# Expert layers of an encoder kernel: splitting the activations before the transposes instead of after them

## The reference, cut to what matters

```python
def swiglu(x, w1, w3, w2):
    return (jax.nn.silu(x @ w1) * (x @ w3)) @ w2

for e in range(N_EXPERTS):          # 8 experts, EXPERT_DIM = 3584
    out = out + combine[..., e:e + 1] * swiglu(x, w1[e], w3[e], w2[e])
```

## Time and profile before

| | |
|---|---|
| median of three runs | 2157.66 us |
| profiled execution, its own time | 2154.84 us |
| its span | 2152.8 us |
| PE busy | 2107.4 us (98%) |
| DVE busy | 1684.3 us (78%) |
| ACT busy | 1323.0 us (61%) |
| granted TensorE clock, mean | 0.988 of full speed |
| experts, from the first to the last transpose | 1083.7 to 2093.2 us |
| one pass of an expert | 127.2 us |

### The profile page before, as it was taken

The page is one execution under the profiler, slowest core; times in us unless marked ns, Lnnn a source line. Parts: engine busy times, 40 slices in busy tenths (PEclk is TensorE's granted clock), DMA queues, the critical chain, the costliest instruction groups (busy, mean ns, idle before and its releaser), DMA issues.

```text
span 2152.8 us, 37035 instructions
## 1 busy us (share of the span) xinstructions
PE 2107.4 (98%) x13496; PEld 1888.2 (88%) x13496; DVE 1684.3 (78%) x2376; ACT 1323.0 (61%) x1864; POOL 24.2 (1%) x45
## 2 busy tenths in 40 slices
PE   8999999899999999999899999999999999999997
PEld 7999999899999999999888888888888888888886
DVE  4998766655457998766588888998888898888885
ACT  5546654444445456545377777777777777777773
POOL 0000100000000000100000000000000000000000
PEclk9999999999999999999899999999999999999999
DMA  7535435355355434453489898998989889898971
GB/s 253 192 116 170 147 135 218 139 214 191 121 197 165 173 118 152 147 196 118 155 320 365 333 350 333 350 365 334 354 341 347 342 341 371 325 356 335 347 305 77
DMA packets 74964, 533.17 MB, mean 248 GB/s; under 512 B 8655, under 2 KB 8655, under 8 KB 11000
## 3 DMA queue, kind: packets, MB, share of 16 engines
q1 hardware_dynamic: 72620, 525.04, 64.2%
q0 software_dynamic: 2048, 6.29, 1.6%
q10 hardware_dynamic: 204, 0.54, 0.1%
HBM read 530.74 MB, written 1.10 MB: 247 GB/s over the span
## 4 chain that ended last, share of the span: by engine, by line
PE 95%; DVE 3%; ACT 1%; DMA 1%; issue 0%; SPq 0%; DVEq 0%; ACTq 0%
PE ps L887 28%; PE ps L889 28%; PE ps L888 28%; PE ps L557 4%; PE ps L1069 1%; PE ps L1098 1%; PE ps L841 1%; PE ps L869 1%; PE ps L753 1%; PE ps L856 1%; DVE xn L1719 0%; DMA constants_sb<-constants 0%; DVE rstd L1713 0%; DVE wlo L2105 0%; PE ps L563 0%; DMA ring<-w_ple 0%
## 5 line engine op out<-in xcount | busy, mean ns | idle before, releaser
L2105 DVE TENSOR_TENSOR wlo<-ring,whi 128x1024 fp32r<-128x1024 f32 x746 | 872.6, 1219 | 144.1 <-ACT whi L1540 143.6
L1540 ACT ACTIVATE whi<-ring 128x1024 fp32r<-128x1024 f32 x746 | 749.3, 1055 | 141.4 <-PE ps L889 130.6
L887 PE MATMUL ps<-whi,xhi 128*128 128x512 f32 (+1 forms) x1160 | 439.4, 379 | 1.0 <-DVE xlo L2227 1.0
L889 PE MATMUL ps<-whi,xlo 128*128 128x512 f32 (+1 forms) x1160 | 430.0, 371 | 0.0
L888 PE MATMUL ps<-wlo,xhi 128*128 128x512 f32 x904 | 356.8, 395 | 0.0
L887 PE MATMUL ps<-xhi,whi 128*128 128x256 f32 x960 | 272.3, 284 | 2.2 <-DVE gt L2127 1.4
L888 PE MATMUL ps<-xlo,whi 128*128 128x256 f32 x960 | 268.0, 279 | 0.0
L889 PEld LDWEIGHTS ps<-whi,xlo 128*128 128x128 f32 x1160 | 219.0, 189 | 40.5
L889 PE MATMUL ps<-xhi,ring_lo 128*128 128x256 f32 x896 | 251.5, 281 | 0.0
L887 PEld LDWEIGHTS ps<-whi,xhi 128*128 128x128 f32 x1160 | 219.4, 189 | 35.6 <-DVE xlo L2227 1.4
L888 PEld LDWEIGHTS ps<-wlo,xhi 128*128 128x128 f32 x904 | 170.3, 188 | 35.9
(11 more groups left out here) (298 smaller groups left out, 3801.3 us busy)
## 6 DMA issues: line engine op xcount, KB each, us to landing
ring<-w_experts SPq DMA_DIRECT2D x340, 1024.0 KB, 4.9
ring<-w_mixers SPq DMA_DIRECT2D x114, 1024.0 KB, 4.9
ring<-w_dense SPq DMA_DIRECT2D x33, 1024.0 KB, 4.8
ring<-w_ple SPq DMA_DIRECT2D x10, 1024.0 KB, 4.9
bias<-bias_rows POOLq DMA_DIRECT2D x8, 256.0 KB, 7.0
cvfa<-bias_rows POOLq DMA_DIRECT2D x8, 256.0 KB, 5.4
constants_sb<-constants SPq DMA_DIRECT2D x1, 1048.0 KB, 9.0
h<-x_in SPq DMA_DIRECT2D x1, 1024.0 KB, 4.9
```

The lines of the kernel that those rows point to most:

```text
L887: pe.matmul(dst, lhs[0], rhs[0], start=first, stop=False, skip_group_check=True)
L889: return pe.matmul(dst, lhs[1], rhs[0], start=False, stop=last, skip_group_check=True)
L1540: act.activation(whi[:, slot, :], ring[:, j % RING, lo:lo + UNIT], ACT.Copy).then_inc(s_wh, 1)
L2105: dve.tensor_tensor(wlo[:, slot, :], ring[:, j % RING, lo:lo + UNIT], whi[:, slot, :], ALU.subtract).then_inc(s_wl, 1)
```

## The change

The hidden values are split before the transposes, by slot: ACT copies `hid` to `hid_high` in fp32r, DVE subtracts to get `hid_low`. PE then turns both by ordinary fp32r products with a unit matrix (`ident_r`), four of 128 moving columns, instead of the two fp32 transposes. One ACT copy of 128 x 512 takes both parts out of PSUM; the subtraction `hlo` from PSUM is gone. The PE waits on `s_hm` and `s_hl` become waits on `s_sl` and `s_hb`. ACT now waits for `s_hm` between units 0 and 1, and DVE for `s_sh` before unit 0.

```diff
-        hhi = sb("hhi", [P, 2, 2, SEQ], F32R)
-        hlo = sb("hlo", [P, 2, 2, SEQ], F32R)
+        hhl = sb("hidden_high_low", [P, 2, 2, 2, SEQ], F32R)
+        hhi, hlo = hhl[:, 0, :, :, :], hhl[:, 1, :, :, :]
+        hid_high = sb("hidden_high_by_slot", [P, SEQ], F32R)
+        hid_low = sb("hidden_low_by_slot", [P, SEQ], F32R)
+        ident_r = sb("ident_r", [P, P], F32R)
...
@@ PE, step
                             if u == 1:
-                                pe.wait_ge(s_hm, c0 + k + 1)
-                                for half in range(2):
-                                    m = pe.transpose(bank(2 + cc % 2, half * P, P), gt[:, 0, half * P:half * P + P],
-                                                     con("ident"))
+                                pe.wait_ge(s_sl, c0 + k + (1 - DENSE_CHUNKS))
+                                for part in range(2):
+                                    for half in range(2):
+                                        m = pe.matmul(bank(2 + cc % 2, part * SEQ + half * P, P),
+                                                      (hid_high, hid_low)[part][:, half * P:half * P + P],
+                                                      ident_r[:, :], start=True, stop=True)
                                 m.then_inc(s_ht, 1)
...
-                        pe.wait_ge(s_hl, c0 + k + 1)
+                        pe.wait_ge(s_hb, c0 + k + (1 - DENSE_CHUNKS))
@@ ACT, route
+                act.activation(ident_r[:, :], con("ident"), ACT.Copy).then_inc(s_id, 1)
@@ ACT, chunk
-                        highs(u0 + (k * 6 + 4), 2, 2, rr, j)
+                        high(u0 + (k * 6 + 4), 2, 0, rr, j)
+                        act.wait_ge(s_hm, c0 + k + 1)
+                        act.activation(hid_high[:, :], hid[:, 0, :], ACT.Copy).then_inc(s_sh, 1)
+                        high(u0 + (k * 6 + 4), 2, 1, rr, j)
...
-                        act.activation(hhi[:, cc % 2, :, 0:P], bank(2 + cc % 2, 0, SEQ).rearrange(
-                            "p (h t) -> p h t", h=2), ACT.Copy).then_inc(s_hh, 1)
+                        act.activation(hhl[:, :, cc % 2, :, 0:P], bank(2 + cc % 2).rearrange(
+                            "p (a h t) -> p a h t", a=2, h=2), ACT.Copy).then_inc(s_hb, 1)
@@ DVE, chunk
                         dve.tensor_tensor(hid[:, 0, :], hs[:, 0, :], bank(cc % 2, SEQ, SEQ), ALU.mult).then_inc(s_hm, 1)
+                        dve.wait_ge(s_sh, c0 + k + (1 - DENSE_CHUNKS))
+                        dve.tensor_tensor(hid_low[:, :], hid[:, 0, :], hid_high[:, :], ALU.subtract).then_inc(s_sl, 1)
                         lows(u0 + (k * 6 + 4), 2, 2, j)
-                        dve.wait_ge(s_hh, c0 + k + 1)
-                        dve.tensor_tensor(hlo[:, cc % 2, :, 0:P], bank(2 + cc % 2, 0, SEQ).rearrange(
-                            "p (h t) -> p h t", h=2), hhi[:, cc % 2, :, 0:P], ALU.subtract).then_inc(s_hl, 1)
```

More of the change, by code:

```diff
@@ L381, in trunk_program @@
         s_ht = sem("hidden_transposed")
+        s_sh = sem("slot_hidden_high")
+        s_sl = sem("slot_hidden_low")
+        s_id = sem("ident_rounded")
+        s_hb = sem("hidden_parts_by_feature")
         s_hh = sem("hidden_hi")
@@ L1082, in experts @@
                     up_unit(0, u, 0, DENSE_UNITS)
+                pe.wait_ge(s_id, 1)
                 with pe.Fori(0, n_p) as q:
```

## The result

The changed kernel takes 2192.62 us (four runs, 2192.03 to 2194.36), the kernel before 2156.05 us (four runs): 1.0174 times as long, 95% interval 1.0162 to 1.0186. The forecast was 2193 us. The profiled execution took 2192.73 us, 37.9 more than the one before (2154.84).

What follows compares the result with a forecast made beforehand. PE's stream was taken to bound the expert stretch. Products 25.2, waits 9.2 and 2.4, and tail 0.2 sum to 37.0 us on 2154.84; with half of 2.8 added, 2193 us, range 2178 to 2245 (90%).

Steps and rivals of the forecast that it cites:

- What bounds the kernel: Expert stretch of 1010 us: each microsecond of PE's stream counts, ACT and DVE savings nothing; 2.5 us lost to PE's sequencer.
- The pair of transposes: The two fp32 transposes removed from each of 112 chunks: 0.227 us per pair, 0.113 for one.
- The price of a short product: Four new fp32r products per chunk at p = 0.113 us each, set by the weight load; 25.2 us more in all.
- The lower bound (columns): Short product priced by moving columns only: 0.059 us each, 1.0 us more over 112 chunks.
- the upper one (full format): Short product as dear as a full-format one: p = 0.226 us, 75.8 us more; as a rival 2244 us, 16%.
- The factor of four for transpose mode: Skill's claim for FP32, by which a plain fp32 product would cost 0.45 us; the prediction read 0.226 from the trace.
- The hand-over: ACT copy and DVE subtraction before PE's turn: operand 0.96 us later after `gt`; chunk 0 waits 1.15 us, 9.2 us in all.
- Chunk 1: Second chunk of each pass: operand ready 0.3 us late, eight times, 2.4 us; known only within 0 to 0.7.
- The ring in the middle chunks: Closed ring of waits from PE's products through ACT and DVE back to PE: 8.36 us against PE's 8.77, nothing charged.
- The rival C: The ring closes in every chunk, 0.1 to 0.3 us open in 96 further chunks: 2203 to 2222 us, 9%.
- The tail: End of the last pass, through `whi`, `wlo` and a transfer: the longer copy adds 0.2 us.
- The sum: 25.2 + 9.2 + 2.4 + 0.2 = 37.0 us on the profiled 2154.84, with half of 2.8 added: 2193 us.

Runs made afterwards that it cites:

- the run with plain products: Kernel before with a plain fp32 product with the unit matrix in place of each transpose, two per chunk; 2179.44 us, 1.0115 times the kernel before.
- the two halvings: Changed kernel with 64 instead of 128 moving columns in the four products, 2192.31 us; with 64 instead of 128 stationary columns, 2171.03 us.
- the products alone: Changed kernel without the hand-over: DVE writes the fp32r tile directly, all four products turn it, low part left out; 2182.78 us, 1.0122 times the kernel before.
- when it was opened: Changed kernel with two more same-size subtractions into spare tiles ahead of the one PE waits for; 2207.78 us, 1.0244 times the kernel before.
- the hand-over run: Changed kernel with the two old fp32 transposes of `gt` in place of the four products, all waits kept; 2164.08 us, 1.0043 times the kernel before.

## Why the prediction was right

**What bounds the kernel.** Right: all that was lost is PE's stream or PE's waits. ACT's busy time grew by 60 us, and of that only the copy ahead of a waiting PE counts. One reading was wrong: the 2.5 us that the prediction gives to PE's sequencer are waits for `hlo` in chunk 0, as shown above. The change takes them away, a gain of some 1.4 us that no term of the sum has.

**The pair of transposes.** Its 0.227 us fits the run with plain products, which cost twice as much, as worked out.

**The price of a short product.** The step that carried the forecast: p = 0.113 from rows of fp32 products with 16, 64 and 128 moving columns, on the ground that their common part is the load. Measured 0.117, and by the two halvings the load is the ground. 112 x 0.24 is 26.9 us for 25.2 forecast; 1.4 of it returned, since the gap in chunk 0 closed, and 25.5 is what the products alone cost. The lower bound (columns) and the upper one (full format) were both far off, so what chose between them mattered more than either. The section LDWEIGHTS of TensorE: Matmul & The Clock Gate in the Trainium skill gives columns / 1.2 ns for a load, an estimate of 107 and 53 ns for 128 and 64 columns. The runs agree nearly by the distances between loads, 0.108 to 0.112 and 0.057 to 0.062 us, and roughly by the price of a product as taken above, 0.117 and 0.069. The factor of four for transpose mode with FP32 in the section Terms of the same page of the Trainium skill, weighed in the prediction, is refuted here: the runs show 0.227 for the pair and 0.45 for the plain products, a factor of two.

**The hand-over.** Chunk 0 of the second pass, to be set beside the earlier trace rows:

```profile
1216.47 0.42 DVE L2261 TENSOR_TENSOR gt<-gs,ps 128x256 f32<-128x256 f32 x1 [1.16 <-ACT gs L1624]
...
1217.29 0.41 ACT L1627 ACTIVATE hidden_high_by_slot<-gt 128x256 fp32r<-128x256 f32 x1
...
1217.72 0.42 DVE L2263 TENSOR_TENSOR hidden_low_by_slot<-gt,hidden_high_by_slot 128x256 fp32r<-128x256 f32 x1 [0.83 <-ACT hidden_high_by_slot L1627]
...
1218.20 0.30 PEld L1107 LDWEIGHTS ps<-ident_r,hidden_high_by_slot 128*128 128x128 f32 x2 [1.18 <-DVE hidden_low_by_slot L2263]
```

From the start of `gt` to PE's load it is 1.73 us; the prediction had 1.74 (1210.31 to 1212.05), with the copy behind unit 0 as it said. The load waits 1.18 us for 1.15 forecast. Chunk 1 waits 0.5 by its load for 0.3, in the stated 0 to 0.7. But the two waits do not add up to lost time: 8 x (131.75 - 130.45) = 10.4 us for 11.6. Against the products alone, columns 13 and 0 grow by 1.14 and 0.33, together 1.47 for the 1.45 of the prediction, and column 1 gives 0.15 back. The term was oversized because a delay of the load was taken for one of the product.

**The ring in the middle chunks.** Nothing was charged, and nothing is lost: 8.79 with and without the hand-over. The cover is 0.6 us, not 0.4. The rival C also counted 96 chunks in it; only 48 waited when it was opened, because scatters, gather and the start of a pass give slack elsewhere.

**The tail.** The charge of 0.2 us for the longer copy is neither shown nor excluded. From the last load of the last turn to the end it is 59.6 us in both kernels, from the first load of that turn 59.8 and 60.1, which holds the longer turn itself; in the other kernels of this study this stretch takes 57.7 to 60.9 us.

**The sum.** 35.9 us in the passes and 37.9 in all, for 37.0 (36.6 by the medians, where the kernel before came out at 2156.05): the small error of the products (+0.3), that of the waits (-1.2) and 1.6 us from outside the experts partly cancel, so the agreement to half a microsecond is in part luck; the split into some 70% products and 30% waits is not.

## What to carry to other kernels

Before replacing a transpose by cheaper-looking products, count weight loads, and not only moving columns. With a load of 128 x 128, a product of 64 or 128 moving columns cost 0.112 to 0.117 us in fp32r and as much for each of the two records of full fp32, so such a product is priced by its load. At 256 moving columns the formats part: the records of the full-format scatter (L1069) are 0.215 us apart, fp32r products 0.118. When an operand gets one more engine in its way, look for the places where it is only just in time (here the first chunk of a pass), and check the closed ring of waits in the others; both can be worked out from one profile, if a wait that the profile calls "issue" is also checked against what the program waits for there. A wait at the start of a loop is mended by moving its consumer and then whatever that consumer delays, and it pays to look at distances between the same instruction in successive iterations, since sums of waits overstate what is lost.

## What the runs showed of the hardware

A late weight load is not a late product: in the hand-over run 14.0 us of waits of loads cost 8.3 us. Transpose mode is cheaper for fp32r operands (0.089 us for 128 x 128) than for fp32 (0.113), and no account here had foreseen that size. The code ahead of the experts, the same in all kernels but for one small copy, ended up to 4.8 us later in some profiled executions than in others.
